# Gated DeltaNet encoder: per-head decay from cumulated gates through DRAM, inverse returned in two parts, fills and opening regrouped, scores three steps ahead

## What is computed

```python
qkv = silu(causal_depthwise_conv(proj[..., :3 * 1024], conv_w))
g = -exp(a_log) * softplus(a_logit + dt_bias)          # per position and head
g = cumsum(g per chunk of 64)                          # here: over tiles of 128 positions, see below
decay = exp(where(tri, g[:, None] - g[None, :], -inf))
lower = where(strict, (k_beta @ k.T) * decay, 0)
sol = triangular_solve(lower + eye, [v * beta, k_beta * exp(g)])
attn_intra = (q @ k.T) * decay
# over chunks, state S (128 x 128):
v_new = u - w @ S;  o = q_dec @ S + attn_intra @ v_new;  S = S * exp(g_last) + k_dec.T @ v_new
```

## Time and profile before

| | us |
|---|---|
| median of the runs (1418.46 to 1423.2) | 1419.47 |
| the profiled execution, its own time | 1421.69 |
| span of its trace | 1419.9 |
| span not under a busy PE | 56.0 |
| DVE busy | 794.3 |
| ACT busy | 533.0 |
| POOL busy | 252.2 |
| DeltaNet stage, PE's first to last instruction for it | about 5 to 414 |

### The profile page before, as it was taken

One profiled execution on the slowest core, in us unless ns is written; L12 is line 12 of the kernel. 1 busy time (PEld: TensorE's weight loads), 2 busy tenths in 40 slices (PEclk: granted clock), 3 DMA queues, 4 the chain that ended last, 5 costly groups with the idle time before them and its releaser, 6 DMA issues.

```text
span 1419.9 us, 18106 instructions
## 1 busy us (share of the span) xinstructions
PE 1363.9 (96%) x6594; PEld 1123.1 (79%) x6594; DVE 794.3 (56%) x1205; ACT 533.0 (38%) x901; POOL 252.2 (18%) x243
## 2 busy tenths in 40 slices
PE   7789999999899999999999999989999999999998
PEld 5678878888778888888888878758888888888877
DVE  5567777777574343343466677674443434435655
ACT  6444445444154132231334431453322313323344
POOL 3644555453030100000002110001010000000211
PEclk9999999999999999999999999899999999999999
DMA  6233233222323223223322352503322232223221
GB/s 178 62 84 78 57 83 84 55 61 69 99 75 118 90 90 118 89 89 104 103 89 86 93 100 64 119 1 104 116 93 89 89 115 93 89 89 100 85 83 60
DMA packets 168575, 125.67 MB, mean 89 GB/s; under 512 B 35873, under 2 KB 165186, under 8 KB 168514
## 3 DMA queue, kind: packets, MB, share of 16 engines
q1 hardware_dynamic: 167410, 123.01, 29.1%
q10 hardware_dynamic: 1104, 1.84, 0.5%
HBM read 116.96 MB, written 5.25 MB: 86 GB/s over the span
## 4 chain that ended last, share of the span: by engine, by line
PE 77%; DVE 11%; DMA 4%; ACT 3%; issue 2%; DVEq 2%; SPq 1%; POOL 0%; ACTq 0%; POOLq 0%
PE psum L148 21%; PE psum L150 21%; PE psum L149 21%; PE psum L890 2%; DMA xScaled<-inv_blocks 2%; DVE wL L140 2%; ACT wH L132 1%; PE psum L900 1%; PE psum L1917 1%; DVE terms L1166 1%; DMA inv_blocks<-blk 1%; DVE bL L1397 1%; DVEq L1168 1%; DVE hT L1598 1%; DVE acc L1596 1%
## 5 line engine op out<-in xcount | busy, mean ns | idle before, releaser
L148 PE MATMUL psum<-aH,wH 128*128 128x512 f32 x896 | 360.1, 402 | 12.2 <-issue 6.9
L150 PE MATMUL psum<-aL,wH 128*128 128x512 f32 x896 | 350.3, 391 | 0.0
L149 PE MATMUL psum<-aH,wL 128*128 128x512 f32 x896 | 349.6, 390 | 0.0
L140 DVE TENSOR_TENSOR wL<-wRaw,wH 128x2048 fp32r<-128x2048 f32 (+2 forms) x125 | 241.0, 1932 | 128.5 <-ACT wH L132 122.9
L148 PE MATMUL psum<-bH,wH 128*128 128x512 f32 x720 | 285.1, 396 | 2.3 <-DVE pleT L2043 1.6
L150 PE MATMUL psum<-bL,wH 128*128 128x512 f32 x720 | 281.0, 390 | 0.0
L149 PE MATMUL psum<-bH,wL 128*128 128x512 f32 x720 | 280.9, 390 | 0.0
L132 ACT CAST wH<-wRaw 128x2048 fp32r<-128x2048 f32 (+2 forms) x109 | 197.0, 1814 | 219.9 <-PE psum L150 219.9
L148 PEld LDWEIGHTS psum<-aH,wH 128*128 128x128 f32 x896 | 168.8, 188 | 45.6 <-issue 8.4
L150 PEld LDWEIGHTS psum<-aL,wH 128*128 128x128 f32 x896 | 168.5, 188 | 35.9
L149 PEld LDWEIGHTS psum<-aH,wL 128*128 128x128 f32 x896 | 169.0, 189 | 31.9 <-issue 0.5
(11 more groups left out here) (295 smaller groups left out, 1511.2 us busy)
## 6 DMA issues: line engine op xcount, KB each, us to landing
wRaw<-in_mlp_w_up SPq DMA_DIRECT2D x64, 512.0 KB
wRaw<-in_mlp_w_down SPq DMA_DIRECT2D x64, 512.0 KB
wRaw<-in_dn_w_in SPq DMA_DIRECT2D x32, 512.0 KB
wRaw<-in_ple_w_gate SPq DMA_DIRECT2D x16, 512.0 KB
xScaled<-inv_blocks SPq DMA_DIRECT2D x16, 256.0 KB, 3.1
wRaw<-in_sw_w_in SPq DMA_DIRECT2D x16, 256.0 KB
wRaw<-in_sw_w_out SPq DMA_DIRECT2D x16, 256.0 KB
wRaw<-in_dn_w_out SPq DMA_DIRECT2D x8, 384.0 KB
```

The lines of the kernel that those rows point to most:

```text
L140: last = [nc.vector.tensor_tensor(o, r, h_.bitcast(F32), ALU.subtract) for o, r, h_ in zip(*([v if half is None else v[:, half * v.shape[1 ...
L148: nc.tensor.matmul(o, wh, xh, start=first, stop=False)
L149: nc.tensor.matmul(o, wl, xh, start=False, stop=False)
L150: return nc.tensor.matmul(o, wh, xl, start=False, stop=last)
```

## The change

Six edits:

1. **Decay.** The gates cumulated by PE for all heads are copied to SBUF (`gCum`), transposed by PE, copied (`gRows`) and written to a DRAM tensor (`decay_rows`), once. For each head a transfer spreads its row of 512 values over all partitions into `gA`; POOL subtracts the position's own value and takes the minimum with 0; ACT takes the exponential. `decay()` is gone from PE. SP issues the load for the next head at the start of `blocks_sp`.
2. **Inverse in two parts.** `blk_out` and `blk_in` are two semaphores each: the read of the inverse waits for its own write alone, `lower(0)` for the inverse alone, `corner(0)` for the transpose.
3. **Order on SP.** The lower part of `blocks_sp` is `lower_sp`; in the opening it stands ahead of `load_panel(2, 0)`.
4. **Low part and fills.** In steps with a `p`, `prep_lo(n, 1, 1)` stands behind `advance(2)` instead of behind `solved(1)`; the fill before `walk(3)` has 2 units instead of 4, the one after `solve(3)` 3 instead of 2, the one after `update(3)` 2 instead of 1. With `b` present the key product (`gram_kk`) comes ahead of `solve(0)`. In the step without `p`, it stands between `blocks_inverse(4)` and `solved(2)`.
5. **Opening.** Panel 2 is cast ahead of the tanh of the keys, its low part taken ahead of their product; POOL takes the taps of the keys, then head 0's decay, then the taps of the values.
6. **Attention.** `scores` goes three steps ahead.

```diff
+        def cums_act(act):
+            act.wait_ge(gate_cum, 1)
+            nc.scalar.copy(gCum[:].rearrange("p (h t) -> p h t", h=HEADS_A), cums[:, 0]).then_inc(gcum_ok, 1)
+            act.wait_ge(gcumT_done, 1)
+            nc.scalar.copy(gRows[:], bank[4][0:HEADS_A * NT, 0:P]).then_inc(grow_ok, 1)
+        def cums_pe(pe):
+            pe.wait_ge(gcum_ok, 1)
+            nc.tensor.transpose(bank[4][0:HEADS_A * NT, 0:P], gCum[:], ident[:]).then_inc(gcumT_done, 1)
...
+        def load_decay(sp, h):
+            sp.dma_start(work[:, 4, :], growD.ap()[bass.ds(h, 1), :].to_broadcast([P, S])).then_inc(g_in, 16)
+        def blocks_sp(sp, a, more=True):
+            if more:
+                sp.wait_ge(dec_ok, a + 1)
+                load_decay(sp, a + 1)
             sp.wait_ge(blk_ok, a + 1)
             for w in range(2):
-                sp.dma_start(diagonal(invD.ap())[:, w], ...).then_inc(blk_out, 16)
-            sp.wait_ge(blk_out, 32 * a + 32)
+                sp.dma_start(diagonal(invD.ap())[:, w], ...).then_inc(blk_out[w], 16)
             for w, dst in enumerate((inv, invT)):
-                sp.dma_start(dst, whole(invD.ap())[:, w]).then_inc(blk_in, 16)
+                sp.wait_ge(blk_out[w], 16 * a + 16)
+                sp.dma_start(dst, whole(invD.ap())[:, w]).then_inc(blk_in[w], 16)
...
-            for n in range(2, 5):
+            for n in range(2, 4):
                 load_panel(sp, n // 2, n % 2)
+            sp.wait_ge(grow_ok, 1)
+            sp.dma_start(growD.ap().rearrange("h (t p) -> (h t) p", p=P), gRows[:]).then_inc(grow_out, 16)
+            sp.wait_ge(grow_out, 16)
+            load_decay(sp, 0)
             sp.wait_ge(blank_out, 32)
+            lower_sp(sp, 0)
+            load_panel(sp, 2, 0)
             with sp.Fori(0, HEADS_A - 3) as a:
                 blocks_sp(sp, a)
                 load_panel(sp, a + 2, 1)
                 load_panel(sp, a + 3, 0)
+                lower_sp(sp, a + 1)
...
         def gA_pool(pool, h):
+            pool.wait_ge(g_in, 16 * h + 16)
             pool.wait_ge(g_ok, h + 1)
-            nc.gpsimd.tensor_tensor(gA, bm(maskLow[:]), bc(gNext[:]), ALU.mult).then_inc(gA_ok, 1)
+            nc.gpsimd.tensor_tensor(gA, gA, bc(gNext[:]), ALU.subtract)
+            pool.drain()
+            nc.gpsimd.tensor_scalar(gA, gA, 0.0, None, ALU.min).then_inc(gA_ok, 1)
...
-            decay()
             if b is None:
+                pe.wait_ge(grow_ok, 1)
                 gram_kk()
-            pe.wait_ge(ss_ok, 2 * a + 2)
-            solve(0)
-            if b is not None:
+                fill(2)
+                pe.wait_ge(ss_ok, 2 * a + 2)
+            else:
                 gram_kk()
-            update(0)
-            fill(2)
+                pe.wait_ge(ss_ok, 2 * a + 2)
+                solve(0)
+                update(0)
+                fill(2)
...
             update(2)
-            fill(4 if p is not None else 3)
+            fill(2 if p is not None else 3)
             walk(3)
             fill(2)
             solve(3)
-            fill(2 if p is not None else 1)
+            fill(3 if p is not None else 1)
             update(3)
             if p is not None:
-                fill(1)
+                fill(2)
...
-            act.wait_ge(dec_done, a + 1)
-            c_.activation(decT, t4(bank[BY]), ACT.Exp).then_inc(dec_ok, 1)
+            act.wait_ge(gA_ok, a + 1)
+            c_.activation(decT, gA, ACT.Exp).then_inc(dec_ok, 1)
...
             solved(1)
-            prep_lo(dve, n, 1, 1)
...
             blocks_inverse(4)
             if p is None:
+                prep_lo(dve, n, 1, 1)
                 out_early_dve(dve, 0)
             solved(2)
             blocks_inverse(8)
             blocks_out()
             advance(2)
+            if p is not None:
+                prep_lo(dve, n, 1, 1)
...
         def dn_act(act):
-            for b in range(2):
-                taps_act(act, 0, b, first=True)
-                tanh_act(act, 0, b)
+            taps_act(act, 0, 0, first=True)
+            tanh_act(act, 0, 0)
+            taps_act(act, 0, 1, first=True)
+            cums_act(act)
+            prep_hi(act, 2, 0)
+            tanh_act(act, 0, 1)
...
         def dn_dve(dve):
-            for b in range(2):
-                silu_dve(dve, 0, b, 0, False)
+            silu_dve(dve, 0, 0, 0, False)
+            prep_lo(dve, 2, 0)
+            silu_dve(dve, 0, 1, 0, False)
...
         def dn_pool(pool):
             taps_pool(pool, 0, 0)
+            taps_pool(pool, 0, 1)
             gA_pool(pool, 0)
-            taps_pool(pool, 0, 1)
+            taps_pool(pool, 0, 2)
...
-            scores(0, [1])
-            scores(1, [1])
+            for i in range(3):
+                scores(i, [1])
...
-                if i + 2 < ATB:
-                    scores(i + 2, [1] if i < 2 else range(2))
+                if i + 3 < ATB:
+                    scores(i + 3, [1] if i < 1 else range(2))
```

More of the change, by code:

```diff
@@ L305, in hybrid_trunk @@
         blk_ok = sem("blk_ok")
-        blk_out = sem("blk_out")
-        blk_in = sem("blk_in")
+        blk_out = [sem(f"blk_out{w}") for w in range(2)]
+        blk_in = [sem(f"blk_in{w}") for w in range(2)]
         def consts_pool(pool):
@@ L436, in hybrid_trunk @@
         gateT_ok = sem("gateT_ok")
+        gcum_ok = sem("gcum_ok")
+        gcumT_done = sem("gcumT_done")
+        grow_ok = sem("grow_ok")
+        grow_out = sem("grow_out")
+        g_in = sem("g_in")
+        gCum = sbd("gCum", [P, HEADS_A * NT])
+        gRows = sbd("gRows", [HEADS_A * NT, P])
+        growD = nc.dram_tensor("decay_rows", [HEADS_A, S], F32, kind="Internal")
         logits = bank[6][:, 0:NT * GATE_COLS].rearrange("p (t c) -> p t c", t=NT)
@@ L459, in gates_act3 @@
         def gates_act3(act):
+            nc.scalar.activation(gate[:, :, EG_:EL_ + 1, :].rearrange("p h q t -> p q h t"), cums, ACT.Exp).then_inc(gate_e, 1)
+        def cums_act(act):
             act.wait_ge(gate_cum, 1)
-            nc.scalar.activation(gate[:, :, EG_:EL_ + 1, :].rearrange("p h q t -> p q h t"), cums, ACT.Exp).then_inc(gate_e, 1)
+            nc.scalar.copy(gCum[:].rearrange("p (h t) -> p h t", h=HEADS_A), cums[:, 0]).then_inc(gcum_ok, 1)
[4 more added lines that the diff above has]
+            nc.tensor.transpose(bank[4][0:HEADS_A * NT, 0:P], gCum[:], ident[:]).then_inc(gcumT_done, 1)
         def gates_dve(dve):
@@ L627, in diagonal, with lower_sp @@
             return d[:, :, 0:B16 * P].rearrange("w b (r c) -> b w r c", c=P)[:, :, :, 0:B16]
-        def blocks_sp(sp, a):
+        def load_decay(sp, h):
+            sp.dma_start(work[:, 4, :], growD.ap()[bass.ds(h, 1), :].to_broadcast([P, S])).then_inc(g_in, 16)
+        def lower_sp(sp, a):
             lo = lowD.ap().unsqueeze(0)
@@ L656, in dn_sp @@
             dn_out_load(sp, 0)
+            lower_sp(sp, HEADS_A - 2)
             blocks_sp(sp, HEADS_A - 2)
@@ L659, in dn_sp @@
             dn_out_load(sp, 2)
-            blocks_sp(sp, HEADS_A - 1)
+            lower_sp(sp, HEADS_A - 1)
+            blocks_sp(sp, HEADS_A - 1, False)
             dn_out_load(sp, 3)
@@ L854, in update @@
                 nc.tensor.matmul(bank[BO][:, P:2 * P], attT[s][:, n, :], vNew[:], start=True, stop=True).then_inc(av_done, 1)
-            def decay():
-                pe.wait_ge(gA_ok, a + 1)
-                per_tile(lambda t: nc.tensor.matmul(bank[BY][:, rng(t)], gA[:, t, :], maskIncl[:], start=True, stop=True)).then_inc(dec_done, 1)
             def gram_kk():
@@ L886, in lower @@
                 if i == 0:
-                    pe.wait_ge(blk_in, 32 * a + 32)
+                    pe.wait_ge(blk_in[0], 16 * a + 16)
                 else:
@@ L898, in corner @@
                     pe.wait_ge(att_ok, a + 1)
+                    pe.wait_ge(blk_in[1], 16 * a + 16)
                 if i < NL - 1:
@@ L1189, in dn_step_dve @@
             stt(out=work[:, 6, :], in0=bank[BZ], scalar=-1.0, in1=work[:, 7, :], op0=ALU.mult, op1=ALU.mult).then_inc(low_ok, 1)
-            if b is None:
-                prep_lo(dve, n - 1, 0)
             advance(0)
@@ L1255, in dn_step_pool @@
             g.tensor_tensor(decC, decT, bc(cK[:, 1 - s, :]), ALU.mult).then_inc(decC_ok, 1)
-            if b is None:
-                taps_pool(pool, a, 2)
             g.tensor_tensor(decM, decT, bm(maskIncl[:]), ALU.mult).then_inc(decM_ok, 1)
@@ L1280, in dn_pe @@
             gates_pe3(pe)
-            project_pe(pe, 0, 24, UNITS, first=True)
+            project_pe(pe, 0, 24, 28, first=True)
+            cums_pe(pe)
+            project_pe(pe, 0, 28, UNITS, first=True)
             pe.wait_ge(cols_ok, 1)
@@ L1308, in dn_dve @@
         def dn_dve(dve):
-            for b in range(2):
-                silu_dve(dve, 0, b, 0, False)
+            silu_dve(dve, 0, 0, 0, False)
+            prep_lo(dve, 2, 0)
+            silu_dve(dve, 0, 1, 0, False)
+            dve.wait_ge(gcum_ok, 1)
+            g_next_dve(dve, 0)
             dve.wait_ge(gate_e, 3)
```

(1 more changed line is left out.)

7 lines of the change are left out of this document (2 added, 5 removed).

## The result

The changed kernel takes 1436.12 us (median of 5 runs, 1431.18 to 1438.45), the kernel before 1419.47 beside it (1418.46 to 1426.3): ratio 1.0092, 95% interval 1.0064 to 1.012. The forecast was 1431.5, slower. The table of the kernel before ends its range at 1423.2; its slowest run beside the changed kernel took 1426.3. The profiled execution took 1438.45 us, its span is 1436.7, 16.8 more than before.

What follows compares the result with a forecast made beforehand. PE and DVE were taken to set the pace in turn within each head. Terms -0.7 + 7.5 + 4.5 + 0 + 2 - 1.3 = +12.0 on 1421.69 gave 1433.7 us, 1431.5 against the median; 8-in-10 range 1417 to 1439.5.

Steps and rivals of the forecast that it cites:

- the moved half: Six heads: second half of the panel's low part, behind `advance(2)`, comes late for unit 16; 1.25 us a head, +7.5.
- One sign: In a steady head of the changed kernel, DVE waits about 1.8 us before `residual(2)`.
- Seams: Ends of heads at `update(0)`, decay products gone from PE: 0.1 us won at each of seven, -0.7; bound -6.3.
- the contention: Six heads: DVE's `prep_lo` slowed beside POOL's first decay operation, between 0 and 0.7 us; 0.35 a head taken.
- that sign of being wrong: Steady head: the forecast is wrong if `walk(3)` comes sooner after `update(0)` than 16.6 us.
- Return in two parts: At `lower(0)` in the six heads: inverse back some 0.8 us earlier but no longer last, so worth nothing.
- The clock: Six heads: half rate expected in three, each losing about 1.5 us; +4.5 us (0 to 9).
- half rate in every head: Rival: half rate in six heads instead of three and full 0.7 of contention, +6.6 us more, 1438; chance 0.15.
- The last pipelined head: Head without projection: low half makes blocks 0.95 us later, return in parts gives 0.8 back; 0 (-0.9 to +1).
- The opening: Before the first head: PE waits 9.7 us at unit 16, `lower(0)` at 90.2, before 87.91; +2 us (-1 to +4).
- Scores: Attention, scores three steps ahead: +1.1 us in the first steps, -2.4 behind the half-rate stretch; together -1.3 (-6 to +1.5).
- the main term: Six heads, low part's second half moved: 0.9 us a head for order, 0.35 for contention; +7.5 (0 to +9.6).

Runs made afterwards that it cites:

- experiment 1: Changed kernel with `prep_lo(n, 1, 1)` back behind `solved(1)` and fills back to 4/2/1, key product still ahead of `solve(0)`: 1408.43 us, ratio 0.9912.
- experiment 2: Changed kernel with only `prep_lo(n, 1, 1)` put back behind `solved(1)`, fills still 2/3/2: 1416.5 us, ratio 0.9971.
- experiment 3: Kernel before the change with only the moved low part and the new fills added: 1439.69 us, ratio 1.0127.
- experiment 8: E1 with the decay again by PE's products and the key product back behind `solve(0)`, gates' copy and transposition kept: 1407.99 us, ratio 0.9923.
- experiment 5: Changed kernel with POOL taking the next head's decay after the taps of the keys: 1425.55 us, ratio 1.0029.
- experiment 6: Kernel before the change with only the inverse's return in two parts added: 1408.12 us, ratio 0.99.
- experiment 7: E1 with the inverse and its transpose waited for together again, on SP and PE: 1420.78 us, ratio 1.0001.
- experiment 12: E1 with 16 unread products in the opening's filling and two ahead of the scores in attention steps 4 to 12: 1414.15 us, ratio 0.9948.
- experiment 4: Changed kernel with six unread 512-column products before `walk(3)` and four behind it, in the six heads: 1428.42 us, ratio 1.004.
- experiment 10: E1 with the scores two steps ahead again instead of three: 1414.15 us, ratio 0.9951.
- E1: The kernel of experiment 1: changed kernel with the low part and fills put back, all else kept; 1408.43 us, ratio 0.9912.
- experiment 11: E1 with panel 2's cast and low part inside the first step again, SP's and POOL's new order kept: 1414.99 us, ratio 0.9941.

## Why the prediction was right

The sign and the mechanism held: the moved half is late and PE waits at both sides of `walk(3)` (experiments 1 to 3). One sign was missed: DVE was to wait about 1.8 us before `residual(2)` and waited 0.97, because 0.59 of its gain was waited away earlier, in `advance(1)`. Step by step:

- **Seams.** Forecast -0.7. Measured -0.3: the saved products are a longer wait (experiment 8).
- **The moved half.** Forecast +0.9 a head for the order and 0.35 for the contention, 7.5 in all. Measured 22.37 to 23.36 without contention (experiment 5), 0.99, and 0.40 with it; 8.3 in all. `walk(3)` was to come no sooner than 16.6 us after `update(0)` and came after 16.57: 0.06 sooner than before, so by the letter that sign of being wrong was met, and DVE gained nothing worth the name. In the half, 1.61 us beside POOL's subtraction stand against 1.20 with POOL idle. The Trainium skill, "SBUF — State Buffer", Who interferes with whom, says that such a pair of VectorE and GpSimd instructions exclude each other; the half and the subtraction overlap by 0.53 us (252.32 to 252.85), so by that rule it would take 1.74, an estimate, and the trace has 1.61.
- **Return in two parts.** Forecast worth nothing in these heads: held, by experiment 3. What I had mis-sized is the part by itself: 0.8 us sooner as I had it, at least 1.25 by experiments 6 and 7. It decided nothing here, but it is where the gain lay.
- **The clock.** The mis-sized term. Forecast half rate once in three of six heads, +4.5; the profiled execution had it in five: at the waits around `walk(3)` in four, twice for 6.83 us (+2.7 each), and once behind `update(0)`. Together +10.3. The number of heads was a guess and could only be one: the same waits brought half rate in two of six heads in experiment 3. Of the rows it went by, the waits at `lower(0)` that left the clock alone were 1.05 to 1.22 us, not 1.2 to 1.4, and the half rate at 362.84 began 0.4 us before the wait of 2.58 ended. The median lies between the forecast and the rival "half rate in every head" (1438), whose number of heads was nearer and whose contention of 0.7 was not found.
- **The last pipelined head.** Forecast 0, measured -0.6: the return in two parts gave 1.35 (21.8 to 20.4, experiment 6), not 0.8, and the low half took 0.7 back (20.4 in experiment 2 to 21.2). With the half rates at 362.84 and 383.32 that are gone, it is -3.6, which I had given nothing. The first of them went with the wait ahead of it, which fell from 2.6 to 1.1 us: half rate stands there in all four traces with a wait of 2.5 to 2.7 (the kernel before, experiments 3, 7 and 12) and in none of the ten with 1.1 to 1.3. The second, behind `update(0)`, comes in experiments 1 and 4 and not here; that one is luck.
- **The opening.** Forecast +2, `lower(0)` at 90.2, measured +3.6, at 91.5. The steps came late by about as much as each other: keys' product done 56.5 (54.5), lower blocks written 65.3 (63.7), blocks out 79.6 (78), the half done 80.7 (79.2). By the trace it begins earlier: PE stood still ahead of 46.74 (1.47 us, before 1.52), but now ran the units up to the transposition at 51.18 at half rate (46.98 to 50.39), and the copy of it (`gRows`, 51.49) held up the cast on ScalarE, which I had given no time; that this is the whole 1.5 was not tried. The one large wait was right in length (8 to 10, measured 8.9) and 2 us late in place (71.9 to 80.8; forecast 69.5 to 79.2). It is the moved half again: experiment 1, without it, has `lower(0)` at 89.1.
- **Scores.** Forecast -1.3. Like for like -1.1 (experiment 10); the rest of the -2.6 is that half rate took 3.41 us here and 10.24 before.

In sum the profiled execution came out 4.7 above the forecast for it (1438.45 against 1433.7): the clock +5.8, the opening +1.6, the main term +0.8, the end +1.0, the seams +0.4 against -3.6 at and behind the last head and -1.3 in attention. So the distance of 4.7 is small partly by luck: misses of 9.6 one way and 4.9 the other.

## What to carry over

Where a wait moves from a transfer to an engine, price the new order of units before the engine that is late: the first unit that needs the moved operand, and when that engine reaches it. Wait for each of two transfers where its data are read, not for both where the first is: this one edit gave 1%, edit 4's low part and fills took 1.8% away, and the others brought nothing that the medians show. Work taken out of an engine that waits for another at the end of that stretch turns into waiting; look there first.

## What the runs showed of the hardware

- Two waits of PE of 1.65 and 1.10 us with 0.46 us of work between them were followed by 3.41 or 6.83 us at half rate (1.2 instead of 2.4 GHz) in four of six heads of the changed kernel and in two of six in experiment 3; waits of 1.64 and 0.70 (experiment 5) or 1.64 alone (experiment 2) in none of six. One wait of 2.5 to 2.7 us, ahead of the last pipelined head's `lower(0)`, had half rate at its end in four traces of four, one of 1.1 to 1.3 in none of ten. One traced execution each.
- The same code in the attention core (scores three ahead) had 0, 3.41 or 20.48 us at half rate in different kernels (111.8 us in experiment 4, 113.2 in the changed kernel, 118.4 in E1). The runs of E1 alone spread from 1405.57 to 1416.95. Medians of experiments 10 and 11 are 5.7 and 6.6 us above E1's where the traces show 1.1 and 0.3, so differences of that size need the traces.
- POOL's TENSOR_SCALAR of 128x512 took 2.27 us where it started beside DVE's L140 (changed kernel) and 1.49 or 1.50 where it did not (E1, experiment 5): the contention costs both.
